# Value stage of an expert layer: running sum of the gathered columns kept in PSUM, low parts of the weight blocks made by GpSimd

## The reference, cut to what matters

```
coef = (gate * gelu(dot(x_t, u[expert]))).astype(x.dtype)   # 8 heads x 16 = 128 slots per token
ffn[t] = sum over the 128 slots of coef[t, slot] * v[expert[t, slot]]   # v has 16384 rows of 2048
h = layer_norm(ALPHA * h + ffn, ln2_g, ln2_b)
```

## Time and profile before

| | |
|---|---|
| median of 3 runs | 2700.19 us (2696.8 to 2708.31) |
| profiled execution, span | 2693.9 us |
| around that span | 2.9 us to the lowest run, 6.3 us to the median |
| value stage, first to last matmul | 2193.47 to 2677.00 us: 483.5 us for 128 steps |
| layer norm and output behind it | 17 us |
| TensorE, VectorE, ScalarE, GpSimd busy over the span | 87%, 72%, 48%, 75% |

### The profile page before, as it was taken

One profiled execution on the slowest core, in us unless ns is written; L12 is line 12 of the kernel. 1 busy time (PEld: TensorE's weight loads), 2 busy tenths in 40 slices (PEclk: granted clock), 3 DMA queues, 4 the chain that ended last, 5 costly groups with the idle time before them and its releaser, 6 DMA issues. The chain is left out here.

```text
span 2693.9 us, 40868 instructions
## 1 busy us (share of the span) xinstructions
PE 2347.5 (87%) x14075; PEld 2088.1 (78%) x14075; DVE 1929.2 (72%) x2948; ACT 1299.5 (48%) x2278; POOL 2015.4 (75%) x1033
## 2 busy tenths in 40 slices
PE   7998999999999999999999878882334479999996
PEld 7997888888888888999988767872323268888885
DVE  4998652623514417456515999989999899999998
ACT  4456455454454454343443012327997844444442
POOL 4887888888888887778783566777788547778773
PEclk9999999999999999999999988985555599999998
DMA  7552555565555554555454999999999969999996
GB/s 234 173 173 94 187 172 187 187 187 187 187 187 187 185 185 160 174 196 172 157 172 172 413 401 395 413 420 422 389 421 421 377 219 385 384 382 375 370 379 252
DMA packets 231586, 722.93 MB, mean 268 GB/s; under 512 B 17388, under 2 KB 53796, under 8 KB 198304
## 3 DMA queue, kind: packets, MB, share of 16 engines
q1 hardware_dynamic: 168416, 356.03, 39.0%
q0 software_dynamic: 57344, 360.74, 33.0%
q10 hardware_dynamic: 5696, 4.47, 0.5%
HBM read 717.51 MB, written 3.67 MB: 268 GB/s over the span
## 5 line engine op out<-in xcount | busy, mean ns | idle before, releaser
L476 POOL TENSOR_TENSOR w_lo<-raw,w_hi 128x1024 fp32r<-128x1024 f32 x464 | 1129.2, 2455 | 253.5 <-ACT w_hi L1199 251.7
L1199 ACT CAST w_hi<-raw 128x1024 fp32r<-128x1024 f32 x464 | 483.9, 1050 | 620.4 <-PE bank L618 409.0
L616 PE MATMUL bank<-B,w_hi 128*128 128x512 f32 x1280 | 454.5, 400 | 15.8 <-DVE B L1799 9.7
L616 PE MATMUL bank<-A,w_hi 128*128 128x512 f32 x1280 | 450.3, 397 | 1.4 <-DVE A L1812 1.4
L618 PE MATMUL bank<-B,w_lo 128*128 128x256 f32 x1280 | 359.4, 281 | 0.0
L618 PE MATMUL bank<-A,w_lo 128*128 128x256 f32 x1280 | 358.4, 280 | 0.0
L1944 DVE TENSOR_TENSOR sq<-bank,T 128x256 f32<-128x256 f32 x128 | 54.1, 425 | 410.4 <-ACT T L1395 410.1
L621 PE MATMUL bank<-A,w_hi 128*128 128x256 f32 x1152 | 330.9, 287 | 6.6 <-POOL w_lo L476 2.9
L570 POOL DMA_INDIRECT vrows<-in_peer_v,ering x192 | 264.7, 1379 | 87.3 <-DVE rest L2359 46.6
L622 PE MATMUL bank<-A,w_hi 128*128 128x256 f32 x1152 | 327.2, 284 | 0.0
L623 PE MATMUL bank<-A,w_lo 128*128 128x256 f32 x1152 | 327.1, 284 | 0.0
(11 more groups left out here) (352 smaller groups left out, 5212.7 us busy)
## 6 DMA issues: line engine op xcount, KB each, us to landing
raw<-in_mlp_w SPq DMA_DIRECT2D x128, 1024.0 KB, 5.2
v_raw<-in_peer_v SPq DMA_DIRECT2D x128, 672.0 KB, 7.4
raw<-in_w_in SPq DMA_DIRECT2D x40, 1024.0 KB, 5.0
raw<-in_cc_w_in SPq DMA_DIRECT2D x64, 512.0 KB, 4.7
raw<-in_cc_w_out SPq DMA_DIRECT2D x16, 1024.0 KB, 5.0
raw<-in_w_out SPq DMA_DIRECT2D x16, 1024.0 KB, 5.1
raw<-in_peer_wq SPq DMA_DIRECT2D x8, 1024.0 KB, 11.5
wq_t<-in_peer_wq SPq DMA_DIRECT2D x2, 2048.0 KB, 24.1
```

The lines of the kernel that those rows point to most:

```text
L476: nc.gpsimd.tensor_tensor(w_lo[:, s % 4], raw[:, s // 2, 2 * (s % 2):2 * (s % 2) + 2, :], w_hi[:, s % 4].bitcast(F32), ALU.subtract).then_ ...
L616: nc.tensor.matmul(bank[m][:].rearrange("p (s t) -> p s t", s=2), wh, both[:, :, kt, :], start=(kt == 0), stop=False)
L1199: nc.scalar.copy(w_hi[:, s % 4], raw[:, s // 2, 2 * (s % 2):2 * (s % 2) + 2, :]).then_inc(hi_done, 1)
```

## The change

The accumulator of the gathered columns moves to a PSUM tensor of two banks, `rest_sum` (704 of 1024 columns; the banks `misc[2]` and `misc[3]` are now views of it). Slot 0 of a half reads `rest` and writes `rest_sum`; slots 1 to 126 read and write `rest_sum`; slot 127 writes `rest`. As the coefficients of the second half stood in `misc[3]`, VectorE copies them out before the loop, where ScalarE did it during the loop.

`weights_low` goes from VectorE to GpSimd. There it is put in front of each pair of rows: `weights_low(n)`, then the rows that replace rows 2(n-1) and 2(n-1)+1. The last three stand behind the last rows.

```diff
-        misc = [psum(f"misc{m}") for m in range(4)]
+        misc = [psum(f"misc{m}") for m in range(2)]
+        late_pair = ctx.enter_context(nc.psum_tensor("late_pair", [P, 1024], F32))
+        misc += [late_pair[:, 0:512], late_pair[:, 512:1024]]
+        rest_sum = late_pair[:, 0:REST]
...
+            def weights_low(first, n):
+
+                pool.sem_inc(passed, 1)
+                pool.wait_ge(ghi_ok, first + (n + 1))
+                pool.sem_inc(passed, 1)
+                low, high = (g[:, n % 2].rearrange("p t (q n) -> p (t q) n", q=PARTS) for g in (g_lo, g_hi))
+                nc.gpsimd.tensor_tensor(low, wmat[:, :, bass.ds(first + n, 1), :].rearrange("p t o n -> p (t o) n"),
+                                        high.bitcast(F32), ALU.subtract).then_inc(glo_ok, 1)
+
+            def weights_and_rows(Q, first, half):
+
+                for m in range(RING // 2):
+                    weights_low(first, 4 * half + m - 3)
+                    value_rows(Q, half, 2 * m, 2)
...
             value_rows(V_FIRST, 0, V_ROWS, RING - V_ROWS)
+            weights_low(0, 0)
             value_experts(1, 1, 0)
-            value_rows(V_FIRST + 1, 1, 0, RING)
+            weights_and_rows(V_FIRST + 1, 0, 1)
...
                         value_experts(2 * r + half, half, t)
-                        value_rows(2 * r + (half + V_FIRST), half, 0, RING)
+                        weights_and_rows(2 * r + (half + V_FIRST), 8 * r, half)
+            for i in range(KEYS - 3, KEYS):
+                weights_low(0, i)
...
-            act.wait_ge(coefT_ps, 2 + PARTS)
-            nc.scalar.copy(coef[:, 1, :], misc[3][:, 0:P]).then_inc(coefT_ok, 1)
...
-                V.scalar_tensor_tensor(rest[:, t, :], vrow[j], coef[:, t, n % SLOTS:n % SLOTS + 1],
-                                       rest[:, t, :], ALU.mult, ALU.add).then_inc(row_used, 1)
+                before = rest[:, t, :] if n % SLOTS == 0 else rest_sum
+                after = rest[:, t, :] if n % SLOTS == SLOTS - 1 else rest_sum
+                V.scalar_tensor_tensor(after, vrow[j], coef[:, t, n % SLOTS:n % SLOTS + 1],
+                                       before, ALU.mult, ALU.add).then_inc(row_used, 1)
...
+            dve.wait_ge(coefT_ps, 2 + PARTS)
+            V.tensor_copy(coef[:, 1, :], misc[3][:, 0:P]).then_inc(coefT_ok, 1)
+            dve.wait_ge(coefT_ok, 2 + PARTS)
 
             for i in range(KEYS):
-                if i == KEYS // NT:
-                    dve.wait_ge(coefT_ok, 2 + PARTS)
-                weights_low(i)
                 gathered(2 * i)
```

More of the change, by code:

```diff
@@ L2345, in value_low @@
                                 ALU.subtract).then_inc(vlo_ok, 1)
[L2347 to L2352, removed]
             def gathered(n):
```

## The result

The changed kernel takes 2739.95 us (median of four, 2737.89 to 2751.26) against 2698.49 us before (four, 2694.29 to 2708.31), measured side by side: ratio 1.015, with 1.0129 to 1.017 as its 95% interval. It is 41 us slower; 52 were forecast.

What follows compares the result with a forecast made beforehand. Before the change, TensorE and VectorE going round together bound the value stage. Forecast: 529 + 3.6 + 3 - 483.5 = +52 on the profiled 2693.9, giving 2746, plus 6.3 to the median: 2752 us; 8-in-10 range 2722 to 2825.

Steps and rivals of the forecast that it cites:

- The likeliest case: Value stage: TensorE waits for GpSimd's g_lo, 4.0 to 4.3 us a step, 2735 to 2775 us; chance 0.55.
- chain of two steps: Value stage, matmul to matmul through v_hi, v_lo, held gather and g_lo: 8.05 us for two steps, 4.03 each.
- The mean step: Value stage: 4.13 us a step, with the copy adding 0.4 to one of four; 128 steps make 529 us.
- GpSimd fits: Rival, value stage: GpSimd's wait costs nothing, TensorE runs unbroken at 3.62 us a step, 2683 us; chance 0.10.
- The price of the pass: The subtraction g_lo on GpSimd, 256 columns: 0.74 us, bounds 0.59 and 1.27.
- The additions: VectorE's additions of 704 columns, sum in PSUM: 0.91 us estimated against 0.946, taken as no change.
- the dependence between them: VectorE, neighbouring additions: the second waits for what the first wrote, 0.2 us a step back.
- TensorE's idle time: Sign, value stage: TensorE idle 0.4 to 0.5 us a step ahead of its matmuls, released by GpSimd's g_lo.
- The other signs: Value stage: DMA share under 1; gathers 0.94 us, or 1.3 to 2.0 with the long ones all inside v_lo.
- The start: Start of the value stage: g_lo(0) stands behind two gathers, TensorE starts 3.6 us later, bounds 3 and 4.3.
- Late rows: Rival half, value stage: late gathered rows push v_lo, about 4.45 us a step, 2793 us; chance 0.20 for both halves.
- The other half: Same rival, VectorE: v_lo meets g_lo in each step, about 4.45 us a step, 2793 us; chance 0.20 for both halves.

Runs made afterwards that it cites:

- no-copy kernel: The changed kernel with GpSimd's loop written out and gathers reading `eid` directly, without the copy to `ering`: 2730.05 us, ratio 1.0157 to before.
- the kernel with the new order: The kernel before with VectorE's order g_lo, v_lo, addition, addition instead of g_lo, addition, v_lo, addition: 2691.91 us, ratio 0.9988.
- pass-only kernel: The changed kernel with the running sum left in SBUF, so only the subtraction g_lo moves to GpSimd: 2831.62 us, ratio 1.0535 to before.
- two-sum kernel: The kernel before with order g_lo, v_lo, addition, addition, even slots summed in SBUF, odd in PSUM: 2692.94 us, repeated 2689.57, ratio 0.9982 both times.

## Why the prediction was right, point by point

**The likeliest case came in**, with its mechanism; what remains are sizes. Its chain of two steps, followed from the first matmul of the step ahead of the slow one shown above:

```profile
2408.30 0.50 PE L1190 MATMUL bank<-v_hi,g_hi 128*128 128x512 f32 x1
...
2411.41 1.05 ACT L1690 CAST v_hi<-v_raw 128x1024 fp32r<-128x1024 f32 x1 [2.22 <-PE bank L1192]
...
2413.16 1.56 DVE L2363 TENSOR_TENSOR v_lo<-v_raw,v_hi 128x1344 fp32r<-128x1344 f32 x1 [0.45 <-ACT v_hi L1690]
...
2413.80 1.74 POOL L573 DMA_INDIRECT vrows<-in_peer_v,ering  x1 [0.30 <-issue]
...
2415.54 0.76 POOL L589 TENSOR_TENSOR g_lo<-wmat,g_hi 128x256 fp32r<-128x256 f32 x1
...
2416.36 0.50 PE L1190 MATMUL bank<-v_hi,g_hi 128*128 128x512 f32 x1
```

That is 3.11 to v_hi, 1.71 on ScalarE, 0.04, v_lo 1.56, the gather 0.82 past it, g_lo 0.76, and 0.06 to the matmul: 8.06 where 8.05 was forecast, and the no-copy kernel's pairs of 8.05 to 8.1 show it without the copy. The kernel with a shorter v_lo shows what the chain hangs on, though that edit also relieves VectorE. That the mean step came so near to the forecast is in part luck: steps that begin with a held gather, three of four, average 4.17, above the forecast, and the quick ones, which it didn't have, pull the mean down to 4.10.

**The mean step** was the term that was mis-sized: 4.10 measured, late rows included, where 4.13 were summed and 3 us kept for late rows on top. The loop from first to last matmul is 523.4 us against 529 + 3, the 2.8 of the clock (below) included. The prediction took the closing of the chain as proof that every step goes that way. In 22 of 126 steps no gather is held and the step is about 3.62, the rival "GpSimd fits", which thus holds for a sixth of the steps. The copy shifts GpSimd into these; its own 0.1 a step is 0.04 to 0.08.

**The price of the pass**: its median is 742 ns, 0.74 taken. Its mean is 820, as it too is held when it starts inside v_lo (17 times), a case that the chain as written didn't have. The gap behind it is 0.16 us, not the 0.30 seen between gathers.

**The additions** were costed right (951 ns, no change), and the dependence between them too (3.72 in the kernel with the new order). VectorE's idle time of more than 0.5 us a step is there: 70 us in 127 before v_lo alone.

**TensorE's idle time** ahead of line 1190 was put at 0.4 to 0.5 us a step, with g_lo as its releaser. The releaser is right, but the rows show 0.26 a step behind the start, a sign that came out weaker than stated. The rows count from a matmul's modelled end: in the slow step they show 0.23 while the step is 0.50 longer than 3.62. The other signs came as forecast: the DMA share is 0.95 and 0.98, and no gather of the stage that starts outside v_lo is over 0.99.

**The start** was put at +3.6 us; from the first g_hi it is +2.85. The second gather was to be held inside v_lo(1), but that one began only at 2198.09 and the gather ran its 0.95. The start has a consequence that the prediction missed: TensorE has then been idle for 3.5 us, and the first step runs at 0.63 us a matmul. In 2200 to 2205 the granted clock averages 0.60. From its first matmul to that of the next step it takes 6.44 us (2198.11 to 2204.55), where an unbroken step is 3.62: 2.8 us are lost in it, 2.4 of them by twelve matmuls that start 0.43 apart instead of 0.226.

**Late rows**, half of a rival, stayed away: landing fell from a median of 7.9 us to 6.5, with fewer bytes moved per us (338 and 363 GB/s against 380 and 394). The other half, VectorE held by the pass in every step, shows in 7 of 128 v_lo; in the kernel with the SBUF sum it is 25.

**The sum against the measurement**, on the profiled executions: 52 forecast, 44.2 measured. The loop gave 8.6 less (with the clock's loss in it), the start 0.75 less; work ahead of the stage came 1.8 later in this execution, and the tail was 0.3 shorter. The other 4 us between 2752 and the measured time are the scatter of the median: 6.3 above the profiled span was taken, and it lay 1.9 above.

## What to carry to other kernels

A mean busy share doesn't say whether an engine can take more work: GpSimd was under 80% busy, but its instructions were held by VectorE's operations with two SBUF inputs, and this was harmless only as long as nobody waited for GpSimd within a step. Before a short operation is moved, follow the chain that its result closes, one round of the buffers long, and count what stands ahead of it in the new queue, waits included. And before handing a full engine's work to a neighbour that it holds up, look for what its own instructions wait for among themselves: two sums instead of one, with a new order, made the stage 8 us shorter here, and with the copy gone as well 11.5, though in the time of the kernel that is 0.3% at best.

## What the runs showed of the hardware

- The exclusion goes both ways and hangs on where the inputs lie. In the changed kernel an indirect DMA's instruction of 0.94 us that starts 0.05 us or more into v_lo ends 0.81 to 0.87 us after it, wherever in it it started; the six that started within its first 0.04 us ran their 0.95 undisturbed. A pass of 0.74 grew to 2.13, a v_lo of 672 columns from 0.86 to 1.90, an addition with both tensors in SBUF from 0.95 to 1.41. An addition with input and output in PSUM and the row in SBUF stays at 942 to 958 ns in all 252 cases, with GpSimd 86% busy beside it. This agrees with the Trainium skill, SBUF — State Buffer, section on the two separate sides, which makes it an exclusive lock held for the whole instruction and names, for VectorE, operations with two SBUF inputs and those in its two-port modes.
- A held gather needs a further 0.82 us after v_lo's end, nearly its whole 0.94, as if it had done next to nothing before. A held pass needs 0.60 of its 0.74.
- The Trainium skill, VectorE: DVE Perf Modes, section on the TRN2 errata, gives an operation from PSUM to SBUF 62 cycles more of fixed cost than one from SBUF to SBUF, by estimate 0.06 us at the clock of its table. For the addition of 704 columns, where one of two tensor inputs moved, no such difference is seen: 946 ns with both in SBUF, 949 with input and output in PSUM, and 933 and 940 for the two in the changed kernel that read PSUM and write SBUF. The measurement decides; a case with PSUM as only input wasn't tried.
- TensorE's clock fell to its lower level of 1.2 GHz at each of the waits of 3.15 us or more ahead of a step that these traces have, before the first matmul in all but one. In that one (the step shown of the pass-only kernel) it fell some 1.6 us after work had begun again, so a wait that is over can still cost matmuls at 0.63 instead of 0.39. It also fell at four waits of 1.8 us in the pass-only kernel and one in the two-sum kernel's repetition, and stayed at 2.4 GHz after one of 2.68 us in the no-copy kernel: the length of the last wait alone doesn't decide it.
